# A fourth score bank and one more unit of look-ahead in two attention stages of an 8-core decoder trunk

## The reference, cut to what matters

```python
# layer 0, differential attention: 4 heads, values 128 wide
a = probs(q1b, k1) - lam * probs(q2b, k2)      # probs: causal softmax(q k / 8)
ob = rms_norm(a @ v, subln) * 0.8
# layer 1, dilated mixture: 16 heads of 64, windows (128, 1), (512, 4), (2048, 16)
alpha = softmax(stack(lses)); out = sum(alpha * outs)
```

## Time and profile before

| | |
|---|---|
| runs | 5443.85, 5533.17 and 5735.37 us, median 5533.17 |
| the profiled execution | 5445.94 us |
| its span, slowest core | 5444.4 us (the cores: 5427.0 to 5444.4) |
| busy share of the span | PE 71%, DVE 43%, ACT 37%, POOL 6% |
| granted clock, mean | 0.793 to 0.799 over the eight cores |
| differential attention | from about 2158 to 2494 us |
| dilated mixture, first group | from about 3889 to 4200 us |
| dilated mixture, second group | from about 4391 to 4700 us |

### The profile page before, as it was taken

How to read it: one execution, slowest core, us unless ns; L and a number is a source line. 1 busy time by engine, 2 the same in 40 slices (tenths; PEclk the granted TensorE clock), 3 DMA queues, 4 the chain that set the end, 5 groups by cost and what they waited for, 6 DMA issues and landing times.

```text
span 5444.4 us, 61792 instructions; the slowest of 8 cores (5427.0 to 5444.4 us)
## 1 busy us (share of the span) xinstructions
PE 3843.1 (71%) x16320; PEld 1541.2 (28%) x16320; DVE 2359.5 (43%) x4259; ACT 2002.8 (37%) x3442; POOL 326.1 (6%) x249
## 2 busy tenths in 40 slices
PE   6999732342531586767989889997666766799986
PEld 2434210010100123223434334343222322234432
DVE  2232466767578544233322332224455445432324
ACT  3231422232331344763322332324455455332323
POOL 0000310000000012000000020001200210000002
PEclk9999765555555568888999889998777878899987
DMA  5343410000000023001433224334200500043422
GB/s 196 124 153 114 135 34 1 0 1 0 0 1 0 1 85 122 1 1 55 169 117 148 106 103 155 116 139 129 78 1 24 153 31 1 32 162 116 159 98 91
DMA packets 83152, 428.89 MB, mean 79 GB/s; under 512 B 9984, under 2 KB 10240, under 8 KB 50048
## 3 DMA queue, kind: packets, MB, share of 16 engines
q1 hardware_dynamic: 82816, 424.94, 22.3%
HBM read 416.52 MB, written 8.39 MB: 78 GB/s over the span
## 4 chain that ended last, share of the span: by engine, by line
PE 54%; DVE 21%; ACT 11%; issue 8%; POOL 3%; DMA 2%; DVEq 1%; SPq 0%; ACTq 0%; POOLq 0%
PE ps L476 11%; PE ps L452 11%; PE ps L448 11%; DVE mk L823 6%; PE ps L668 5%; DVE Ib L799 3%; ACT eb L650 3%; PE ps L646 2%; PE ps L716 2%; PE ps L396 2%; PE ps L511 2%; ACT sqb L393 2%; ACT eb L907 2%; PE ps L642 2%; DVE pb L655 2%
## 5 line engine op out<-in xcount | busy, mean ns | idle before, releaser
L448 PE MATMUL ps<-hn,wbff 128*128 128x512 bf16 x2816 | 678.4, 385 | 28.9 <-ACT wbff L362 28.9
L452 PE MATMUL ps<-hn,wbff 128*128 128x512 bf16 x2816 | 668.5, 380 | 9.7 <-DVE wbff L364 9.7
L458 DVE TENSOR_TENSOR act<-sg,ps 128x512 bf16<-128x512 f32 x352 | 242.2, 688 | 873.7 <-PE ps L452 873.6
L476 PE MATMUL ps<-act,wbff 128*128 128x512 bf16 x2816 | 609.1, 379 | 14.1 <-ACT wbff L362 14.1
L650 ACT ACTIVATE eb<-ps 128x512 bf16<-128x512 f32 x960 | 490.4, 533 | 348.8 <-PE ps L642 143.7
L456 ACT ACTIVATE sg<-ps 128x512 f32<-128x512 f32 x352 | 210.5, 598 | 857.8 <-PE ps L448 782.2
L834 PE MATMUL pTp<-mats,mk 128*128 128x128 bf16 x136 | 18.3, 304 | 630.3 <-DVE mk L827 555.3
L668 PE MATMUL ps<-pb,VG 128*128 128x512 bf16 (+3 forms) x640 | 263.4, 414 | 213.1 <-DVE pb L655 205.7
L448 PEld LDWEIGHTS ps<-hn,wbff 128*128 128x128 bf16 x2816 | 278.2, 99 | 370.9 <-issue 46.6
L452 PEld LDWEIGHTS ps<-hn,wbff 128*128 128x128 bf16 x2816 | 275.6, 98 | 348.5 <-issue 19.6
L476 PEld LDWEIGHTS ps<-act,wbff 128*128 128x128 bf16 x2816 | 275.0, 98 | 348.2 <-issue 17.9
(11 more groups left out here) (132 smaller groups left out, 4432.6 us busy)
## 6 DMA issues: line engine op xcount, KB each, us to landing
wstm<-odd_w_in SPq DMA_DIRECT2D x96, 512.0 KB, 4.3
wstf<-ffn_a_wg SPq DMA_DIRECT2D x44, 1024.0 KB, 6.9
wstf<-ffn_a_wu SPq DMA_DIRECT2D x44, 1024.0 KB, 5.2
wstf<-ffn_a_wd SPq DMA_DIRECT2D x32, 1408.0 KB, 8.6
wstf<-ffn_b_wg SPq DMA_DIRECT2D x44, 1024.0 KB, 7.4
wstf<-ffn_b_wu SPq DMA_DIRECT2D x44, 1024.0 KB, 6.0
wstf<-ffn_b_wd SPq DMA_DIRECT2D x32, 1408.0 KB, 8.9
wstm<-ew_fm SPq DMA_DIRECT2D x72, 512.0 KB, 4.5
```

Source lines behind the costliest of these rows:

```text
L448: A("pe", lambda e, k=k, bg=bg, gt=gt, fi=fi, sub=sub: e.matmul(ps[bg][:], lhsT=gt[:, k, fi * 128:(fi + 1) * 128], rhs=hn[:, k, sub * 512: ...
L452: A("pe", lambda e, k=k, bu=bu, ut=ut, fi=fi, sub=sub: e.matmul(ps[bu][:], lhsT=ut[:, k, fi * 128:(fi + 1) * 128], rhs=hn[:, k, sub * 512: ...
L476: A("pe", lambda e, fc=fc, tl=tl, di=di, sub=sub, b=b: e.matmul(ps[b][:], lhsT=tl[:, fc % 11, di * 128:(di + 1) * 128], rhs=act[:, fc, sub ...
```

## The change

It is in three places. PSUM gets an eighth float32 bank `ps[7]`, and the transposes' tile `pTp` becomes a bfloat16 view of that same bank. `run_units` takes the look-ahead as an argument; differential attention and the mixture pass 3, so AV of unit n stands just before S of unit n + 4, while the sparse attention keeps 2. In the two stages that pass 3, `srot` rotates over the banks 0, 1, 2 and 7, and there are five eb and five pb buffers.

```diff
-        ps = [st.enter_context(nc.psum_tensor(f"ps{i}", [128, 512], F32)) for i in range(7)]
-        pTp = st.enter_context(nc.psum_tensor("pTp", [128, 1024], BF16))
+        ps = [st.enter_context(nc.psum_tensor(f"ps{i}", [128, 512], F32)) for i in range(8)]
+        pTp = ps[7].bitcast(BF16)
...
-        def run_units(units, front, back):
+        def run_units(units, front, back, look=LOOK):
             fr = []
             for idx, u in enumerate(units):
                 fr.append(front(u))
-                if idx >= LOOK:
-                    back(units[idx - LOOK], fr[idx - LOOK])
-            for idx in range(max(0, len(units) - LOOK), len(units)):
+                if idx >= look:
+                    back(units[idx - look], fr[idx - look])
+            for idx in range(max(0, len(units) - look), len(units)):
                 back(units[idx], fr[idx])
...
-        def attn_tiles(f2sb, mengs=("dve", "pool")):
-            ebs = [f2sb(f"eb{i}", [128, 512], BF16) for i in range(4)]
-            pbs = [f2sb(f"pb{i}", [128, 512], BF16) for i in range(4)]
+        def attn_tiles(f2sb, mengs=("dve", "pool"), nslot=4):
+            ebs = [f2sb(f"eb{i}", [128, 512], BF16) for i in range(nslot)]
+            pbs = [f2sb(f"pb{i}", [128, 512], BF16) for i in range(nslot)]
...
-                            ebs = ebs + [f2sb("eb3", [128, 512], BF16)]
-                            pbs = pbs + [f2sb("pb3", [128, 512], BF16)]
-                            erot, prot = Rot(range(4)), Rot(range(4))
-                            srot = Rot([0, 1, 2])
+                            ebs = ebs + [f2sb("eb3", [128, 512], BF16), f2sb("eb4", [128, 512], BF16)]
+                            pbs = pbs + [f2sb("pb3", [128, 512], BF16), f2sb("pb4", [128, 512], BF16)]
+                            erot, prot = Rot(range(5)), Rot(range(5))
+                            srot = Rot([0, 1, 2, 7])
...
-                            run_units(units, dfront, dback)
+                            run_units(units, dfront, dback, 3)
...
-                            tiles = attn_tiles(f2sb, mengs=("dve",))
-                            srot = Rot([0, 1, 2])
+                            tiles = attn_tiles(f2sb, mengs=("dve",), nslot=5)
+                            srot = Rot([0, 1, 2, 7])
...
-                            attn_jobs(jobs, accrot, srot, tiles, kz=kzd)
+                            attn_jobs(jobs, accrot, srot, tiles, kz=kzd, look=3)
```

More of the change, by code:

```diff
@@ L615, in run_units, with attn_jobs @@
                 fr.append(front(u))
-                if idx >= LOOK:
-                    back(units[idx - LOOK], fr[idx - LOOK])
-            for idx in range(max(0, len(units) - LOOK), len(units)):
+                if idx >= look:
+                    back(units[idx - look], fr[idx - look])
+            for idx in range(max(0, len(units) - look), len(units)):
                 back(units[idx], fr[idx])
-        def attn_jobs(jobs, accrot, srot, tiles, kz=None):
+        def attn_jobs(jobs, accrot, srot, tiles, kz=None, look=LOOK):
             ebs, pbs, rds, erot, prot, rrot, mengs = tiles
@@ L680, in back @@
                       r=[("ps", bb), ("rd", di)], w=[dkey])
-            run_units(units, front, back)
+            run_units(units, front, back, look)
         def make_kz(f2sb, nbuf=2):
@@ L695, in make_kz @@
             return kzs, fill
-        def attn_tiles(f2sb, mengs=("dve", "pool")):
-            ebs = [f2sb(f"eb{i}", [128, 512], BF16) for i in range(4)]
-            pbs = [f2sb(f"pb{i}", [128, 512], BF16) for i in range(4)]
+        def attn_tiles(f2sb, mengs=("dve", "pool"), nslot=4):
+            ebs = [f2sb(f"eb{i}", [128, 512], BF16) for i in range(nslot)]
+            pbs = [f2sb(f"pb{i}", [128, 512], BF16) for i in range(nslot)]
             rds = [f2sb(f"rd{i}", [128, 512], F32) for i in range(2)]
-            return (ebs, pbs, rds, Rot(range(4)), Rot(range(4)), Rot(range(2)), Rot(mengs))
+            return (ebs, pbs, rds, Rot(range(nslot)), Rot(range(nslot)), Rot(range(2)), Rot(mengs))
         def apply_wout(w2d, merged):
```

## The result

The changed kernel takes 5344.2 us (median; its runs begin at 5340.8). Against the kernel before the ratio is 0.9812, with a 95% interval of 0.979 to 0.9833: it is 1.7 to 2.1% faster. Against the profiled execution of before, 5445.94 us, that is 102 us less where 72.6 were forecast.

What follows compares the result with a forecast made beforehand. It took a 2.21 us latency loop to bound the mixture and PE to bound differential attention. Mixture 2 x (14.7 + 16.0) plus differential 11.2 gave 72.6 us off 5445.9: 5374 us, range 5325 to 5472, forecast case 0.60.

Steps and rivals of the forecast that it cites:

- What bounds the stages: Mixture's steady loop: a 2.21 us ring of latencies, shared by three units before and four after; PE bounds differential attention's units.
- The rate: Mixture's steady loop: 0.737 us per unit falls to 0.57, with bounds of 0.553 and 0.675.
- The count of steady units: Mixture: 15 units per 32-unit job and 7 per 24-unit job gain, 88 per group, worth 14.7 us per group.
- The mixture's diagonal and job end: Ends of mixture jobs: 1.2 us gained in 12 jobs, 0.4 in four, 16.0 us per group (bounds 0 and 26).
- the clock's rival: Mixture: the clock no longer falls at job ends, 48 us on top of 73, 5325 us; chance 0.13.
- The slow-clock units stay at 0.82: Mixture job starts at the low clock: PE alone sets 0.82 us per unit, so no gain there.
- ACT "is late next": Mixture's steady loop after the change: ACT's 0.53 us per exponential hides the rest, units taken at 0.57.
- the near bound (0.675): Mixture's steady loop: ACT's pace from another stretch, 0.675 us per unit, leaving a gain of 5.5 us per group.
- the rival at 5413 us: Gain stops at ACT's own pace of 0.675 us: 33 us gained in all, 5413 us; chance 0.18.
- Differential attention: Steady units are PE's and gain 0; job ends gain 0.8 us in 12 jobs, 0.4 in four: 11.2 us.
- The finishing chain's stall stays: Mixture job ends: the chain's own 4.5 us without a DVE product stay, its instructions being the same.
- The later chain's rival: Job ends in 15 + 32 jobs: one more exponential ahead of Ln, 0.55 us each, 26 us lost, 5472 us; chance 0.09.

Runs made afterwards that it cites:

- e6: Changed kernel with look-ahead 4 in place of 3 in both stages, same banks and buffers: 5318.2 and 5350.3 us, ratio 0.9789.
- e4: Changed kernel with look-ahead back at 2, four score banks and five buffers kept: 5445.0 us, ratio 0.9999.
- e3: Changed kernel with look-ahead 3 kept, but three score banks and four eb and pb buffers in both stages: 5343.9 us, ratio 0.9816.
- e5: Changed kernel with look-ahead 1 in the mixture, 3 kept in differential attention: spans of 5678 to 5688 us on cores 4 to 7.
- e7: Changed kernel with the six instructions finishing a mixture job handed out behind the next six backs: 5276.0 us, ratio 0.9678.
- e8: The mixture's handed-out job ends, with differential attention's finishing instructions handed out likewise, on the changed kernel: 5237.9 us, ratio 0.961.

## Why the prediction was off, point by point

- **What bounds the stages: right.** A loop of 2.21 us over look-ahead + 1 units. After the change it measures 2.20 us over four.
- **The rate: right.** 0.737 to 0.57 was forecast, 0.167 us per unit; full-clock units gained 0.71 - 0.54 = 0.17 on average.
- **The count of steady units: right.** "88 units per group" were priced at 14.7 us, and these same units gained 15.9.
- **"The mixture's diagonal and job end": wrong in size, and this is the step that failed.** It was put at 16.0 us per group; everything outside the 88 units gained 27.1 (table above), 1.9 us in each of the 12 jobs of 16 to 32 units where 1.2 were taken, 1.0 in the 4 jobs of 8 units where 0.4 were. The prediction's 1.4 us, of which it took 1.2, were one exponential more ahead of the Ln (0.74) and a chain that starts 0.7 earlier. Counted from the job's first 384-wide score, the AV behind the stall comes only 0.27 us earlier on average, but ahead of it stand two scores and one AV more. Behind the stall these three matmuls would cost 1.29 us at the low clock (0.43 each, half of the prediction's 0.86 for two); with the 0.27 that is 1.6 of the 1.7 us that the average job gained, an estimate. One S and one AV of them the prediction named in the clock's rival ("only one S and one AV more to fill 4.27 us"), but its sum gave them nothing, because the stall stays as long. What is done while PE would stand is not paid afterwards, whatever the stall's length.
- **"The slow-clock units stay at 0.82": right for the single unit**, which is 0.85 us behind the stall in both kernels. It is their number that fell: the sixth and seventh scores of a job are no longer among them.
- **ACT "is late next": wrong at look-ahead 3.** ACT's own pace is 0.48 (e6), and it is the bound only at look-ahead 4. The pace of 0.53 in the earlier trace rows belonged to exponentials fed by the loop. This made the near bound (0.675) and the rival at 5413 us too likely.
- **Differential attention: right in kind, low in size.** 11.2 us forecast, 16 measured. The ends gave 1.0 us per job on average, where 0.8 and, for short jobs, 0.4 were taken; in jobs of 16 and 24 units the distances behind the eight diagonal scores add to 5.1 us before and 4.1 after.
- **Banks and buffers at 0: right**, by e4. I didn't say that they could be left out; e3 shows it.
- **The finishing chain's stall stays: right** (distances of over 3 us add to 79.3 and 79.8 us per mixture group, 106.3 and 107.3 in the differential stage). The clock's rival fell with it: the granted clock of the groups is 0.79 and 0.81 as before. The later chain's rival is a fraction of its price.
- The sum: the mixture's ends are 2 x (27.1 - 16.0) = 22.2 us short, its steady units 2 x 1.2, the differential stage 5; 72.6 + 29.6 = 102.2, the measured 102. (The prediction's 5373.3 is 5373 when rounded, not 5374; nothing hangs on it.) The forecast put 0.82 on a change within 2%, at 1.3%; with the ends priced right its own sum would have been 1.9%, at the edge of what it called measurable.
- **The Trainium skill's price of an activation** ("ScalarE: Activation LUTs", section "What ACT_TABLE_LOAD costs"): with one pointer operand its figures give, as an estimate, 0.61 us back to back, which would have stopped the units there. The trace disagrees with that form: 0.56 in the changed kernel and 0.49 in e6. Its form without a pointer gives 0.52, an estimate too; the 0.49 and the shortest distance of 0.48 in e6 lie under that as well.

## What to carry to other kernels

Where no engine is full, look for the loop: the distance between two equal instructions, divided by the units in it, is the price of one, and one more unit in flight costs a number in the issue order, not a bank, as long as the bank's reader is done by the time the next write stands at the queue's head (e3 holds to that in the steady stretch; at job ends in e3 and e6 PE waits for the bank). Then price the whole job by place, its start and its end as carefully as the steady stretch: here they gave 27 of a group's 43 us. What an engine gets done ahead of a fixed stall counts in full, even if the stall stays as long. What finishes a job is worth handing out between later units: here it gave 68 us in the mixture and 38 in differential attention, together as much as the look-ahead, and the granted clock rose with it.

## What the runs showed of the hardware that was not expected

With look-ahead 1 (e5) the mixture ran at a granted clock of 0.50 to 0.56 over 100 us on end (1.2 GHz nearly all the time). PE had the stalls at job ends there, as before, and between them it stood 0.5 to 0.6 us for a product in about every second unit. With look-ahead 2 and 3 the steady stretch had 1.00 behind stalls that were no shorter (4.9 us from score to score in e5, 5.0 in the other two), and with look-ahead 4, where most of these distances are 3.6 us, the granted clock of a group is 0.76 to 0.79, no higher than before. When the job ends were handed out (e7, e8) it rose to 0.92. What the low clock itself cost in e5 was not tested: look-ahead and clock moved together.
